# Bias lookups with bf16 one-hots and a three-part table, all 24 steps placed by the second quarter's burst

## What is computed

```python
c_act = jax.nn.silu(c)
mod = c_act @ w_mod[l] + b_mod[l]
shift, scale, gate = jnp.split(mod, 3, axis=-1)
h = rmsnorm(x, norm_gain[l]) * (1.0 + scale[:, None, :]) + shift[:, None, :]
proj = h @ w_in[l]
...
bias = rel_bias[t5_bucket(pb[:, :, None] - ps)]     # 32 buckets x 8 heads
logits = jnp.einsum('bqhd,bqkd->bqhk', qb, ks).astype(jnp.float32) * scale + bias
```

## Time and profile before

| | |
|---|---|
| median of 3 runs | 1883.29 us (1882.03 to 1883.4) |
| the profiled execution | 1882.59 us, its span 1880.7 us |
| PE busy | 1839.4 us (98%) |
| DVE / ACT / POOL busy | 1352.0 / 991.8 / 202.1 us |
| read from memory | 418.45 MB, 225 GB/s over the span |
| chain that ended last | PE 92%, DMA 3%, DVE 2%, ACT 2% |

### The profile page before, as it was taken

One profiled execution on the slowest core, in us unless ns is written; L12 is line 12 of the kernel. 1 busy time (PEld: TensorE's weight loads), 2 busy tenths in 40 slices (PEclk: granted clock), 3 DMA queues, 4 the chain that ended last, 5 costly groups with the idle time before them and its releaser, 6 DMA issues.

```text
span 1880.7 us, 24046 instructions
## 1 busy us (share of the span) xinstructions
PE 1839.4 (98%) x9040; PEld 1525.7 (81%) x9040; DVE 1352.0 (72%) x1949; ACT 991.8 (53%) x1359; POOL 202.1 (11%) x256
## 2 busy tenths in 40 slices
PE   5989999999999999999999999999999999999997
PEld 3768788889888878888888888888888888888886
DVE  6979999998987878757756544488875456665555
ACT  6664555546446445544644644566664445443464
POOL 0000002100000000210000000044431020031001
PEclk9989999999999999999999999999999999999999
DMA  9989978965986976744465556554454655657562
GB/s 352 371 317 346 327 241 303 322 215 184 340 290 237 359 256 233 237 157 157 128 223 183 192 187 199 192 169 158 156 173 161 199 180 181 196 182 246 180 195 96
DMA packets 211825, 424.05 MB, mean 225 GB/s; under 512 B 7680, under 2 KB 12684, under 8 KB 210316
## 3 DMA queue, kind: packets, MB, share of 16 engines
q1 hardware_dynamic: 209788, 414.94, 65.4%
q10 hardware_dynamic: 1936, 7.76, 1.0%
HBM read 418.45 MB, written 4.21 MB: 225 GB/s over the span
## 4 chain that ended last, share of the span: by engine, by line
PE 92%; DMA 3%; DVE 2%; ACT 2%; issue 1%; SPq 0%; DVEq 0%; POOLq 0%; POOL 0%; ACTq 0%
PE acc L684 28%; PE acc L686 27%; PE acc L685 27%; DMA raw<-in_w_in 2%; DVE scr L2074 1%; DMA raw<-in_w_mod 1%; PE tps L725 1%; PE sps L1076 1%; PE tps L765 1%; ACT w_hi L1414 0%; PE sps L893 0%; PE sps L892 0%; ACT proj L1389 0%; PE sps L996 0%; PE tps L988 0%
## 5 line engine op out<-in xcount | busy, mean ns | idle before, releaser
L1855 DVE TENSOR_TENSOR w_lo<-raw,w_hi 128x1024 fp32r<-128x1024 f32 (+1 forms) x580 | 721.1, 1250 | 456.2 <-ACT w_hi L1242 453.9
L1242 ACT ACTIVATE w_hi<-raw 128x1024 fp32r<-128x1024 f32 (+1 forms) x580 | 606.7, 1050 | 773.8 <-PE acc L686 692.9
L684 PE MATMUL acc<-w_hi,ht_hi 128*128 128x512 f32 (+1 forms) x2304 | 910.3, 395 | 0.5 <-issue 0.4
L686 PE MATMUL acc<-w_hi,ht_lo 128*128 128x512 f32 (+1 forms) x2304 | 894.1, 388 | 0.0
L685 PE MATMUL acc<-w_lo,ht_hi 128*128 128x512 f32 (+1 forms) x2304 | 892.3, 387 | 0.0
L686 PEld LDWEIGHTS acc<-w_hi,ht_lo 128*128 128x128 f32 x2304 | 432.4, 188 | 90.2
L684 PEld LDWEIGHTS acc<-w_hi,ht_hi 128*128 128x128 f32 x2304 | 432.8, 188 | 87.3 <-issue 2.9
L685 PEld LDWEIGHTS acc<-w_lo,ht_hi 128*128 128x128 f32 x2304 | 433.3, 188 | 83.3
L1985 DVE SCALAR_TENSOR_TENSOR scr<-raw,vcol,scr 128x512 f32<-128x512 f32 x154 | 110.9, 761 | 4.9 <-issue 0.4
L2074 DVE SCALAR_TENSOR_TENSOR scr<-raw,vcol,scr 128x1024 f32<-128x1024 f32 x56 | 68.1, 1279 | 6.1 <-DMA raw<-in_w_mod 5.9
L1985 DVE SCALAR_TENSOR_TENSOR proj<-raw,vcol,proj 128x512 f32<-128x512 f32 x70 | 52.3, 788 | 1.9
(11 more groups left out here) (305 smaller groups left out, 1475.2 us busy)
## 6 DMA issues: line engine op xcount, KB each, us to landing
raw<-in_w_in SPq DMA_DIRECT2D x208, 1024.0 KB, 5.1
raw<-in_w_mod SPq DMA_DIRECT2D x64, 1024.0 KB, 5.8
raw<-in_w_mod SPq DMA_DIRECT2D x64, 512.0 KB, 6.6
raw<-in_w_out SPq DMA_DIRECT2D x32, 1024.0 KB, 5.2
raw<-in_w_o SPq DMA_DIRECT2D x16, 1024.0 KB, 5.1
raw<-in_w_ple_gate SPq DMA_DIRECT2D x16, 1024.0 KB, 5.1
raw<-in_w_b_out SPq DMA_DIRECT2D x8, 1024.0 KB, 5.2
raw<-in_w_a_out SPq DMA_DIRECT2D x8, 1024.0 KB, 5.1
```

The lines of the kernel that those rows point to most:

```text
L684: pe.matmul(o, hi_m, w_hi[:, slot, u, 0:width], start=start, stop=False)
L686: mm = pe.matmul(o, lo_m, w_hi[:, slot, u, 0:width], start=False, stop=stop)
L1242: act.activation(w_hi[:, x % SPL, :, 0:width], raw[:, j, 2 * (x % halves):2 * (x % halves) + 2, 0:width], ACT.Copy).then_inc(hi_ready, 1)
L1855: dve.tensor_tensor(w_lo[:, x % SPL, :, 0:width], raw[:, j, 2 * (x % halves):2 * (x % halves) + 2, 0:width], w_hi[:, x % SPL, :, 0:width]. ...
```

## The change

It does three things. The one-hots become bf16. The table `rb_diag` is split by POOL, after the same transfers, into three bf16 parts whose sum is the table, and each lookup product becomes three, accumulated in the same place; PE's first use waits for POOL (`rb_split`) instead of the table's transfer. And the steps are placed anew: 5 ahead of the quarters, then 9 in the first quarter (one behind its `w_in` items, two in each slot), 10 in the second (one between, one behind, two in each slot), none in the third and fourth.

```diff
-FIRST_STEPS = 4
-STEPS = [(0, 1, (1, 1, 2, 1)), (1, 1, (1, 1, 2, 1)), (1, 1, (1, 1, 2, 1)), (0, 0, (0, 0, 0, 0))]
+FIRST_STEPS = 5
+STEPS = [(0, 1, (2, 2, 2, 2)), (1, 1, (2, 2, 2, 2)), (0, 0, (0, 0, 0, 0)), (0, 0, (0, 0, 0, 0))]
...
-        onehot = proj[:, 0, 5632:6656].rearrange("p (b n) -> p b n", b=2)
+        onehot = proj[:, 0, 5632:6144].bitcast(BF16).rearrange("p (b n) -> p b n", b=2)
+        rb_parts = proj[:, 0, 5312:5312 + 3 * KPG * NH // 2].bitcast(BF16).rearrange("p (b n) -> p b n", b=3)
+        rb_rest = proj[:, 0, 5248:5248 + 2 * KPG * NH].rearrange("p (b n) -> p b n", b=2)
...
-                        mm = pe.matmul(bias_cols[:, c:c + KPG * NH], onehot[:, n % 2, e * w + m * P:e * w + (m + 1) * P],
-                                       rb_diag, start=True, stop=True)
+                        for b in range(3):
+                            mm = pe.matmul(bias_cols[:, c:c + KPG * NH], onehot[:, n % 2, e * w + m * P:e * w + (m + 1) * P],
+                                           rb_parts[:, b, :], start=b == 0, stop=b == 2)
...
-            pe.wait_ge(s_rb, 16 * KPG)
+            pe.wait_ge(rb_split, 1)
...
+            pool.wait_ge(s_rb, 16 * KPG)
+            link(pool.tensor_copy(rb_parts[:, 0, :], rb_diag))
+            link(pool.tensor_tensor(rb_rest[:, 0, :], rb_diag, rb_parts[:, 0, :], ALU.subtract))
+            link(pool.tensor_copy(rb_parts[:, 1, :], rb_rest[:, 0, :]))
+            link(pool.tensor_tensor(rb_rest[:, 1, :], rb_rest[:, 0, :], rb_parts[:, 1, :], ALU.subtract))
+            pool.tensor_copy(rb_parts[:, 2, :], rb_rest[:, 1, :]).then_inc(rb_split, 1)
```

More of the change, by code:

```diff
@@ L336, in build @@
         rb_zeroed = sem("rb_zeroed")
+        rb_split = sem("rb_split")
         buckets_ready = sem("buckets_ready")
```

## The result

| | before | after |
|---|---|---|
| median (14 runs each) | 1882.86 us (1882.03 to 1884.81) | 1887.81 us (1885.68 to 1889.25) |
| ratio after to before | | 1.0024, 95% interval 1.0016 to 1.0032 |
| the profiled execution, its span | 1882.59, 1880.7 us | 1887.10, 1885.3 us |
| PE's fourth burst begins | 129.79 us | 135.40 us |
| PE busy | 1839.4 us | 1824.0 us |

The kernel is 4.95 us slower by the medians (0.26%; the ratio of the runs gives 0.24%, with an interval wholly above 1), though PE is busy 15 us less. The time lies in the predicted range of 1885 to 1895; the predicted 1890.6 is 2.8 us too high.

A forecast was written before the change was run, and what follows sets the result against it. PE alone bounds from its fourth burst at 129.79 us; before it DVE and DMA pace the quarters. Terms 9.13 - 1.13 - 0.64 = +7.36 us on that start gave 1890.6 us, range 1885 to 1895.

The forecast's parts named there:

- rival 2: Before the fourth burst, transfers that had time to land remove DVE's remaining idle time: +3.3, 1886.6 us; chance 0.13.
- a two-step slot: In the bursts, a slot with two steps takes 2.52 us with one shortened lookup, 2.91 with row turns.
- first `w_hi`, second quarter: ACT stays for slot 4's own spread, so this instruction begins at 69.8 us, 4.67 later than 65.14.
- first `w_hi`, third quarter: The same wait on ACT after the second burst: begins at 102.62 us instead of 93.49, 9.13 late.
- third quarter, `w_hi` to burst: Two steps go from between ACT's `w_hi` and the tiles: 7.99 us instead of 9.12, so 1.13 come back.
- fourth burst against third: DVE's 0.64 us wait for `w_hi` at the fourth quarter's beginning counted as gone, transfers being ahead after the stall.
- two steps in every slot of the first burst: The main term: a second step cannot be prepared, so slot 4 is reached 21.93 us after the burst's start.
- so no lead is lost to it: During DVE's stall, DMA runs full of four landed slots and stops too, losing no lead; no cost counted.
- The fifth early step: Ahead of the quarters, some 2 us more on ACT, counted as nothing; up to 2 us if its cover is gone.
- Rival 1: At ACT's second step in slot 4 the wait is covered, so the kernel is not slower: 1881.3 us; chance 0.08.
- Rival 3: PE idles in four slots; clock falls to 1.2 GHz for one half in each burst: +4.4, 1895 us; chance 0.08.
- Rival 4: Three-part lookups on PE cost more than fp32, 1.2 us each, on six slots: +4.2, 1894.8 us; chance 0.09.

The follow-up runs named there:

- run 1: The kernel after with the steps placed as in the kernel before, so only the lookups change: 1882.00 us against 1882.17 for the kernel before.
- Runs 3 and 4: Kernel after with one step in slot 4 of the first two bursts: 1881.49 us; with only ACT's last step there moved behind the next first `w_hi`: 1884.61 us.
- Run 5: Kernel after with one step in slot 4 of the second burst, the leftover step moved into the third burst: 1884.49 us against 1883.01 for the kernel before.
- run 2: The kernel before with only the new placement of steps, lookups still fp32: 1893.75 us against 1882.17 for the kernel before.

## Why the prediction was right, and what it missed

**The bound.** As predicted: PE is busy without a gap from the fourth burst to 500 us (364.48 of 364.60 us), behind 220 us each matmul is shifted by the same time (below), and all that counts is the start of that burst. That start moved by 5.61 us and the time by 4.95. What stands last in front of it I had read only in part. In all nine kernels ACT's `w_hi` of both items of the fourth quarter begins on a transfer's landing (121.80 us before, 127.41 after, 5.61 apart), DVE waits for the second item (0.34 to 0.36 us, 0.07 in run 1), and the burst follows 7.98 to 8.00 us after the first. So a stall of ACT and DVE in an earlier quarter reaches the time as transfers that are asked for and land later.

**The mechanism.** As predicted: two steps in slot 4, ACT behind the burst, DVE behind ACT, in two quarters. Runs 3 and 4 show it from two sides, one by PE's and ACT's table, one by ACT's order alone. By the number alone the result stands nearer to rival 2 (1886.6) than to the forecast (1890.6); it is the two `w_hi` rows behind a `Relu` that tell them apart.

**The terms of the sum.**

| term | predicted | measured |
|---|---|---|
| first burst begins | 46.1 | 45.83 us |
| its first half, mostly at 1.2 GHz | 5.04 | 4.69 us |
| a two-step slot (with row turns) | 2.52 (2.91) | 2.24 (2.63) us |
| slot 4 of the first burst | 68.0 | 66.54 us |
| first `w_hi`, second quarter | +4.67 | +3.18 us (68.32) |
| first `w_hi`, third quarter | +9.13 | +6.06 us (99.55) |
| third quarter, `w_hi` to burst | -1.13 | -1.58 us (7.54 instead of 9.12) |
| fourth burst against third | -0.64 | +1.13 us (28.31 instead of 27.18) |
| start of PE's gapless stretch | +7.36 | +5.61 us |

The size is off mainly by the step "two steps in every slot of the first burst", its lookup. I took 0.5 us for what is 0.31, and 0.82 for what it replaced, though on the path it is 0.91: a two-step slot lost 0.60 us, not 0.32. Over three slots that is 0.84 us in each of two bursts. My range had 0.3 us as the lower end, and I had chosen a value between the ends. The row that I started from (128 columns, 57 ns a pair) was set by its columns and not by its load, as the same load with 32 columns shows at 26 ns. The Trainium skill, "TensorE: Matmul & The Clock Gate", section "Wait — 56ns, not 53.3ns?", says that starts are never less than about 25 ns apart; that would have given 0.3 us for twelve, and the 26 ns a pair agree with it. The same page's formula in "LDWEIGHTS (loading the stationary operand)" gives 107 ns for a load of 128 columns. The trace records each of these loads as 96 ns long, but they begin 26 ns apart, so the formula does not give what a load costs in a row of such pairs. The other part is the first half at 1.2 GHz: 4.69 and 4.28 us (77.41 to 81.69) instead of 5.04 twice. The clock rose sooner into the burst; in all kernels here that half takes 4.3 to 5.3 us, and I had one value. (In the first burst the granted clock reads 1.00 throughout. That PE is slow there is read from its products, one every 0.43 us until 51.0 in the kernel before. They are as far apart from 74.8 to 78 us, where the granted clock is 0.50, and 0.23 us apart where it is 1.00.)

**The step that failed** is in the same paragraph: "so no lead is lost to it". The prediction says this of the transfers. While DVE stands, the two `w_in` slots are not freed, the two items behind them land, and no new one is asked for between 64.7 and 71.8 us. The transfers fell to 181 GB/s from 70 to 74 us:

```profile
70.00:74.00 4.00, 2.05 (x21) 1.45 (x20) 3.10 (x5) 3.97 (x6) 0.00 (x0) 0.53 0.61 181
```

DVE then ran on what had landed, until the deficit came due: 0.41, 0.81 and 0.23 us of waits at 118.7, 122.0 and 124.7, ahead of the fourth quarter's `w_hi`. So the wait of 0.64 us that I had counted as gone was replaced by others twice as long. Run 5, with one hole, has its waits on transfers mostly one quarter sooner (94.07, 101.49). Its third quarter's `w_hi` begins on a landing 3.28 us later than before (96.77 against 93.49), its fourth's 3.21 later (125.01 against 121.80): the transfers did not make up what one stall had cost them. That the deficit is the cause rests on these two placements and the rates; I have no run that keeps the stall and refills the slots. The errors of the sum, +3.1 (the third quarter's `w_hi`), +0.45 (from there to the burst) and -1.8 us (fourth burst against third), make the 1.75 us between 7.36 and 5.61. So two errors partly cancel: with the waits on transfers as I had them, the sum would have been 3.5 us too high. Another 0.66 us of the 2.8 came back behind the start of the fourth burst (below), and 0.43 is the base, 1883.29 us from three runs against 1882.86 from fourteen.

**The covers.** POOL's five instructions ended at 12.08 us, long before PE's first spread, which the new wait stands ahead of (17.64), and its first lookup (23.7):

```profile
11.87 0.21 POOL L2595 CAST proj<-proj 128x32 bf16<-128x32 f32 x1
```

The fifth early step cost nothing here (first `w_hi` at 37.27, on a transfer), as predicted, but the cover was as thin as said: with fp32 lookups it broke and cost 1.15 us (run 2).

**The rivals.** Rival 1 would have needed the second step for nothing; it did not come. Rival 2, the quarters making it up, went the other way. Rival 3: the products after each slot ran at full speed in the kernel after, 2.83 to 2.86 us a half. The clock did fall behind a slot once, in run 1, and cost nothing there. Rival 4: the lookups became cheaper, not dearer.

**From the fourth burst to the end** 0.74 us came back (by the last matmul; by the medians 0.66). I put this down to chance timing and not to the change: with the same table of steps 0.5 us came back in run 2, and with the same lookups 1.7 us were lost in run 1. Aligning the same matmul of each kernel, the shift stays constant to within 0.1 us for the last 1650 us and jumps only twice ahead of it: in the fourth burst, by when the clock reaches 2.4 GHz (-0.2 for the kernel after, +0.8 for run 1, +1.1 for run 5), and in the index stage (-0.4 to -0.8 us in seven of the eight kernels compared with the one before, +0.9 in run 1). There PE does small products on 64 rows in two groups of four with a wait before each. In the kernel before, the second group came late: its first load waited 0.25 us for DVE (L2166).

```profile
211.40 0.48 PE L892 MATMUL sps<-scr 64*128 64x128 f32 x2
...
212.16 0.49 PE L892 MATMUL sps<-scr 64*128 64x128 f32 x2
...
213.01 0.66 PE L884 MATMUL tps<-kst,proj 128*128 128x128 f32 x4
```

in the kernel after both were ready, and the two groups ran interleaved:

```profile
216.86 0.50 PE L896 MATMUL sps<-scr 64*128 64x128 f32 x3
...
217.31 0.59 PE L897 MATMUL sps<-scr 64*128 64x256 f32 x3
...
217.84 0.66 PE L888 MATMUL tps<-kst,proj 128*128 128x128 f32 x4
```

From the first of the eight to the next transposes 1.61 us before (211.40 to 213.01) and 0.98 after (216.86 to 217.84): a gain of 0.63 us. Why DVE was late in the one and not in the other is not shown.

## What to carry to other kernels

A producer-consumer step squeezed in as filler has a place in the line of every engine it touches: before putting two in a slot, look which later instruction of the slowest path stands behind its last part on an in-order engine, and keep the last slot's step one whose input was already issued. A stall of the consumer also stops the buffers from being freed; count the transfers not started in it, since here they came due one or two stages later. And read GB/s beside the DMA share before calling the transfers full.

## What the hardware showed that I had not expected

- A bf16 pair of load and 32-column matmul starts every 26 ns at full clock, 0.31 us for 12, against 0.91 us for the eight fp32 matmuls on the path. At a granted clock of 0.50 it is 27 ns (the twelve at 71.69 us), while the row of eight fp32 ones goes from 0.98 to 1.92 us (51.87 and 100.10 us in the kernel before).
- DMA share 1.00 with 355 GB/s and share 1.05 with 385 GB/s in the same kernel family, at the same sizes of packets; what lowers the rate in the bursts of the kernel before stays open.
- Two fp32 products on different halves of the rows ran at the same time when the second had nothing left to wait for: two groups of four that took 1.61 us one after the other took 0.98 us. The Trainium skill, "TensorE: Matmul & The Clock Gate", section "Part 3: Packing small matmuls — row/col tiling", states this for different row groups; the rows above agree.
